# One 128-wide spreading product instead of two 64-wide ones in neighbourhood attention

## The chip, the cores and the metric

The kernel runs on one core of a Trainium2 chip. The metric is the time of one execution in device microseconds (us); three runs of the kernel before give a median of 941.36 us. Besides them one execution was recorded by the hardware profiler; all rows below come from it. Engines are named as in the profile: PE is TensorE's matrix products, PEld its weight loads (the stationary operand), DVE is VectorE, ACT ScalarE, POOL GpSimd, SP SyncE.

## What is computed

Two transformer-like blocks over 512 tokens of width 1024. The second block has two layers; in each, half of the width goes through neighbourhood attention: tokens stand on a grid of 8 rows by 64 columns, and each of 8 heads (head size 64) attends to a window around its token. Cut to what matters:

```python
logits = einsum('bhcd,bhicjd->bhcij', qr, kr) * scale + bias
p = softmax(logits)                      # over the keys of the window
out_a = einsum('bhcij,bhicjd->bhcd', p, vr)
...
y = concatenate([out_a * silu(g_a), out_b * silu(g_b)])
x = x + y @ w_out[l]
```

The kernel does not divide the probabilities by their sum. It weighs the values with the unnormalised exponentials, and multiplies the result, together with the gate, by the reciprocal of the sum. The result has the head's 64 channels on the partitions and 128 tokens along the free axis, while the reciprocals stand as one column of 128 tokens on the partitions. So they have to be turned and repeated over 64 partitions, which an identity product does.

## The kernel before

Neighbourhood attention of one layer is 16 steps `m` (`N_NA` = 16), each a pair of heads for 128 queries and 256 keys (`KW`); `M = 16 * l + m` counts over both layers. Three steps are begun early, inside the projections before; the others run in a software pipeline written out by hand, where turn `j` of each engine holds:

- PE: `na_score(j)`, three products (high and low parts of q and k) for each of two heads; the head size of 64 is contracted, so one head uses the upper 64 rows of the array and the other the lower 64. Then `na_turn(j - 2)`, four 128x128 transposes of the exponentials. Then `na_weigh(j - 3)`: four value products with 64 output columns (two heads, two key halves), a wait on `na_rinv`, and two spreading products, one for each head, also 64 columns wide: the stationary operand is the reciprocal column broadcast to 64, the moving one the identity.
- DVE: `na_take(j)` (adds the bias to the scores, finds the maximum), `na_inverse(j - 1)` (the reciprocals of two sums), and every other turn `na_out`, `na_lo`, `na_hi` (gate times reciprocal times result, and its split in two parts); at j = 6, 8, 10, 12 also `mixT_lo`, a 128x512 subtraction.
- ACT: `na_move(j - 2)` (transposed exponentials out of PSUM), then `na_exp(j)` (two exponentials with their sums).

Everything is ordered by semaphores, each engine running its own list in order. `settle` makes the engine wait for the instruction just issued. An fp32 product of PE, here the value and the spreading products, is two entries in the trace; a transpose is one; a score product, whose operands are fp32r, is one. `soft,v` and `soft,xn_t` are the tiles of the value products, `cons,ring` of the transposes, `cons,small` of the spreading products, `k_hi,q_hi` and its like of the scores. In the trace nearly all products have line 1023, a helper's.

Another part of each layer, differential attention, has scores of the same kind, transposes (line 1364) and value products that are 128 columns wide (`v,soft`).

Of the kernel before, what the change touches and what calls it, by code (L numbers as in the profile page):

```python
# [11 lines left out]
P = 128  # L12
# [3 lines left out]
NH, HD, NG = 8, 64, 2  # L16
# [11 lines left out]
KW = 32 * GROWS  # L28
# [40 lines left out]
def build(nc, io):  # L69
# [8 lines left out]
    with ctx:  # L78
# [3 lines left out]
        def sb2(name, n, dtype=fp32):  # L82
            return second.enter_context(nc.sbuf_tensor(name, [P, n], dtype))
# [4 lines left out]
        def cut(view, **dims):  # L88
            return view.rearrange("p (" + " ".join(dims) + ") -> p " + " ".join(dims), **dims)
# [44 lines left out]
        hT_hi, hT_lo = (cut(sb2(n, KD * T, fp32r)[:, :], k=KD, t=T) for n in ("hT_hi", "hT_lo"))  # L134
        w_hi, w_lo = (cut(sb2(n, 4 * UNIT, fp32r)[:, :], u=4, n=UNIT) for n in ("w_hi", "w_lo"))

        prob2 = cut(ring[:, 0:SLOT], b=8, t=T)
        tanh2 = cut(ring[:, 0:NT * 512], i=NT, f=512)
        raw_w = cut(ring[:, SLOT:2 * SLOT], u=4, n=UNIT)
# [12 lines left out]
        def row(name):  # L152
            return rows[:, ROWS[name][0]:ROWS[name][1]]

        def con(name):
            return cons[:, CONS[name][0]:CONS[name][1]]
# [7 lines left out]
        ident = con("ident")  # L164
# [58 lines left out]
        def stat(n):  # L223
            sm_at[0] += n
            assert sm_at[0] <= 640
            return small[:, sm_at[0] - n:sm_at[0]]
# [10 lines left out]
        ssum = stat(16)  # L237
        rinv = stat(16)
# [89 lines left out]
        def p_raw(n):  # L328
            return piece(ring, n)
# [77 lines left out]
        def na_bank(m):  # L407

            return bank[4 + m // 2 % 2]
# [608 lines left out]
        def _(pe):  # L1018
# [3 lines left out]
            def mm(out, lhsT, rhs, first, last):  # L1022
                return pe.matmul(out, lhsT, rhs, start=first, stop=last)  # L1023


            def times_c(out, w, ks=range(KD)):
                for k in ks:
                    r = k % 4 * 32
                    ins = mm(out[r:r + 32, :], csl_pad[:, k, :], w[:, k, :], k < 4, k >= 4)
                return ins  # L1030
# [9 lines left out]
            for c in range(4):  # L1040
                if c < 2:
# [4 lines left out]
                    for i in range(2 * c, 2 * c + 2):  # L1046
                        pe.wait_ge(S["xn_ready"], i + 1)
                        for b in range(2):
                            if i:
                                pe.wait_ge(S["xT_evac"], 2 * i + b - 1)  # L1050
                            for k in range(4):
                                ins = pe.transpose(bank[6 + b][:, k * P:(k + 1) * P], xn[:, i % 2, (4 * b + k) * P:(4 * b + k + 1) * P], ident)
# [4 lines left out]
                else:  # L1057
                    for n in range(2):
                        pe.wait_ge(ada_late_in[1 + n], 16)
                        ins = times_c(bank[c], ada_late[1], range(4 * n, 4 * n + 4))  # L1060
# [59 lines left out]
            for k in range(KD):  # L1120
                pe.wait_ge(S["h_raw"], k + 1)
                ins = mm(bank[0][:, :], p_raw(0)[:, k, :], hT[:, k, :], k == 0, k == KD - 1)
# [15 lines left out]
            for n in range(8):  # L1138
# [3 lines left out]
                for a in range(4):  # L1142
                    g = 4 * (n % 4) + a
                    ins = pe.transpose(bank[4 + n % 4][:, a * P:(a + 1) * P], src[:, g * P:(g + 1) * P], ident)
# [6 lines left out]
            for n in range(2):  # L1151
                for b in range(4):
                    for a in range(4):
                        g = 8 * a + 4 * n + b
                        ins = mm(bank[4 + n][32 * a:32 * a + SC, b * P:(b + 1) * P], b_st[:, g, :], cl3[:, g, 0:P], True, True)
# [5 lines left out]
            for part, w in enumerate((wi, wr)):  # L1161
                if part:
                    pe.wait_ge(S["kk_evac"], 2)
                for g in range(GP):
                    for two in range(2):
                        ins = mm(bank[6 - 2 * part + g // 8][two * SN:(two + 1) * SN, (g % 8) * NCH:(g % 8 + 1) * NCH],
                                 w[:, g, two * SN:(two + 1) * SN], u_in[:, 2 * g + two, :], True, True)
# [46 lines left out]
            for n in range(4):  # L1214
# [6 lines left out]
                for a in range(8):  # L1221
                    g = 2 * (8 * q + a) + two

                    out = bank[4 + n][:, a * NCH:(a + 1) * NCH]
# [3 lines left out]
                    for half_ in halves:  # L1228
                        ins = mm(out[half_, :], cl3[:, g, SC:SC + P][:, half_], st[:, g, :], False, True)
                ins.then_inc(S["y_done"], 1)  # L1230

            for f in range(4):
# [3 lines left out]
                if f == 2:  # L1236
# [5 lines left out]
                    for m in range(2):  # L1242
                        ins = mm(bank[5][0:64, 0:HD], hk[:, 0, m, :], w2k[:, m, :], m == 0, m == 1)
                    ins.then_inc(S["kc_done"], 1)
                    for g in range(NG):
                        for m in range(2):
                            for h in range(2):
                                half_ = slice(h * SN, (h + 1) * SN)
                                ins = mm(bank[6][half_, g * HD:(g + 1) * HD], vdup[:, m, g, half_], w2v[:, m, :], m == 0, m == 1)
# [47 lines left out]
            for f in range(4):  # L1297
                if 1 <= f < 3:
                    pe.wait_ge(S["proj_evac"], PT_ZA + f)
                out, cs_ = bank[GLU_BANKS[f]][:, :], slice(f * P, (f + 1) * P)  # L1300
# [8 lines left out]
                for k in range(4):  # L1309
                    if f == 0:  # L1310
                        pe.wait_ge(S["h_lower"], KD + k + 1)
                    ins = mm(out, glu_w_hi[:, k, cs_], y_lo[:, k, :], False, k == 3)
# [33 lines left out]
            for n in range(2):  # L1346
                for a in range(4):
                    o = (4 * n + a) * P
                    ins = pe.transpose(bank[n][:, a * P:(a + 1) * P], soft[:, o:o + P], ident)
# [61 lines left out]
            n = len(PAIRS1)  # L1411
# [31 lines left out]
            def tile_T(out, l, g, f):  # L1443

                u = first_unit(l, g) + f
                pe.wait_ge(S["w_split"], u + 1)
                for k in range(KD):
                    w = [unit_shape(v, u)[:, k, :] for v in (w_hi, w_lo)]
                    ins = mm3(out[:, :], w, (hT_hi[:, k, :], hT_lo[:, k, :]), k, k == 0, k == KD - 1)
                return ins  # L1450

            def tile_tok(out, l, g, i, order=range(KD), between=None):

                tok = slice(i * P, (i + 1) * P)
                for m, k in enumerate(order):
                    u = first_unit(l, g) + m // 2
                    if m % 2 == 0 and i == 0:
                        pe.wait_ge(S["w_split"], u + 1)
                    if m == 4 and between:
                        between()  # L1460
                    w = [unit_shape(v, u)[:, m % 2, :] for v in (w_hi, w_lo)]
                    ins = mm3(out[:, :], (hT_hi[:, k, tok], hT_lo[:, k, tok]), w, k, m == 0, m == KD - 1)
                    if m in (1, 3, 5) and i == NT - 1:
                        ins.then_inc(S["w_used"], 1)
                return ins
# [59 lines left out]
            def na_weigh(l, m):  # L1525
                i, p = PAIRS_NA[m]
                M = N_NA * l + m
                pe.wait_ge(S["na_moved"], M + 1)
                if m % 2 == 0 and M >= 4:
                    pe.wait_ge(S["na_out"], M // 2 - 1)  # L1530
                src, b0 = ((v2, 0), (v_mid, 0), (v_mid, 1), (v2, 2))[i]
                out = na_bank(m)
                for b in range(2):
                    for e in range(2):
                        hf = slice(e * HD, (e + 1) * HD)
                        mm(out[hf, m % 2 * P:(m % 2 + 1) * P], src[:, b0 + b, (2 * p + e) * HD:(2 * p + e + 1) * HD],
                           probT2[:, m % 4, e * KW + b * P:e * KW + (b + 1) * P], m % 2 == 0 and b == 0, False)
                pe.wait_ge(S["na_rinv"], M + 1)
                for e in range(2):
                    hf = slice(e * HD, (e + 1) * HD)  # L1540
                    r = (2 * M + e) % 16
                    ins = mm(out[hf, KW + m % 2 * P:KW + (m % 2 + 1) * P], rinv[:, r:r + 1].to_broadcast([P, HD]), ident, False, m % 2 == 1)
                ins.then_inc(S["na_weighed"], 1)

            for l in range(LAYERS):
                for half in (1, 0):
# [15 lines left out]
                    for g in range(4 - 4 * half, 8 - 4 * half):  # L1562
                        for t in range(4):
# [6 lines left out]
                            if KINDS[g] not in BY_TOKENS:  # L1570
                                ins = tile_T(bank[p % 4], l, g, t)
                            elif (g, t) == (0, 1):
                                ins = tile_tok(bank[p % 4], l, g, t, between=lambda: (rows_T(l, 2), rows_T(l, 3)))
                            else:
                                ins = tile_tok(bank[p % 4], l, g, t)
# [3 lines left out]
                            if (g, t) in MIX_TURNS:  # L1579
                                m = MIX_TURNS.index((g, t))  # L1580
# [11 lines left out]
                    if half:  # L1592
                        for j in range(N_EARLY, N_DA + LAG_O):
# [5 lines left out]
                            if LAG <= j < N_DA + LAG:  # L1599
                                m = j - LAG  # L1600
                                turn(u0 + m, prob_of(k0 + 2 * m), NT, "mixed", u0 + m + 1)
                            if j >= LAG_O:
                                m = j - LAG_O
# [32 lines left out]
        def _(dve):  # L1636
            steps = [0]

            def settle(ins):
                ins.then_inc(S["vec_step"], 1)  # L1640
                steps[0] += 1
                dve.wait_ge(S["vec_step"], steps[0])
# [10 lines left out]
            def wide_b(v, n):  # L1653

                return v.unsqueeze(2).to_broadcast([v.shape[0], v.shape[1], n])
# [184 lines left out]
            for l in range(LAYERS):  # L1840
                sl = slice(l * HD, (l + 1) * HD)
                for m, (a, b) in enumerate((("lq1", "lk1"), ("lq2", "lk2"))):
                    ins = dve.tensor_tensor_reduce(kc_sb[:, 0:HD], row(a)[:, sl], row(b)[:, sl], 1.0, 0.0, MUL, ADD,
                                                   lam_t[:, 2 * l + m:2 * l + m + 1])
# [127 lines left out]
            for m in range(2):  # L1972
                ins = dve.tensor_copy(vdup[:, m, :, :].rearrange("p g (u j) -> p g u j", u=4),
                                      src[:, 1, m, :, :].unsqueeze(2).to_broadcast([P, NG, 4, NCMP]))
# [34 lines left out]
            for g in range(NG):  # L2009
                for q in range(4):  # L2010
                    ins = dve.tensor_copy(vblk[q * 32:(q + 1) * 32, g, q * HD:(q + 1) * HD],
                                          bank[6][q * 32:(q + 1) * 32, g * HD:(g + 1) * HD])
# [92 lines left out]
            n = len(PAIRS1)  # L2105
# [129 lines left out]
            def na_inverse(l, m):  # L2235
                M = N_NA * l + m
                dve.wait_ge(S["na_exp"], 2 * M + 2)
                if M >= 8:
                    dve.wait_ge(S["na_weighed"], M - 7)
                r = slice(2 * M % 16, 2 * M % 16 + 2)  # L2240
                dve.reciprocal(rinv[:, r], ssum[:, r]).then_inc(S["na_rinv"], 1)

            def na_out(l, g):
                dve.wait_ge(S["na_weighed"], N_NA * l + 2 * g + 2)
# [16 lines left out]
            for l in range(LAYERS):  # L2261
                for half in (1, 0):
# [75 lines left out]
                    else:  # L2338
                        for j in range(N_EARLY, N_NA):
# [9 lines left out]
                            if j - MIX_LAG in MIX_AT:  # L2349
                                m = MIX_AT.index(j - MIX_LAG)  # L2350
                                mixT_lo(l, m, 4 + m, mixT[m])
                        na_inverse(l, N_NA - 1)
                        for g in range(N_NA // 2 - 2, N_NA // 2):
                            na_out(l, g)
# [118 lines left out]
```

## Time and profile before

| what | value |
|---|---|
| median of three runs | 941.36 us (941.17 to 942.0) |
| the profiled execution, whole | 941.23 us |
| its span, first to last instruction | 939.4 us |
| mean granted TensorE clock | 0.996 |
| neighbourhood attention's pipeline, layer 1 | 564.15 to about 591.8 us |
| the same, layer 2 | 860.75 to about 888.4 us |

The profiled execution is 0.13 us off the median of the others, so sums made against it hold for the median too. The span leaves out 1.8 us before the first and after the last instruction.

A row of the timeline gives start in us, duration in us, engine, line, operation, output and inputs by name, the array mode (rows*columns in use) for PE, the shape, and how many neighbouring entries are merged. For merged entries the duration runs from the start of the first to the end of the last. Ends of products are modelled; starts are what to read. Brackets give idle time before the row and what ended it.

### The profile page before, as it was taken

The page shows a single profiled execution, that of the slowest core. Times are in us where ns is not written, and L with a number is a line of the kernel's source. Part 1 is how long each engine was busy: PE and PEld are TensorE (multiplying, and loading weights), DVE is VectorE, ACT ScalarE, POOL GpSimd, SP SyncE. Part 2 cuts the span into 40 slices and gives each one's busy share as a digit, 9 for nine tenths or more (in the row PEclk, how much of TensorE's full clock was granted, in tenths as well). Part 3 has the DMA queues.
Part 4 walks back from the last instruction along what each step waited for, and adds up shares of the span by engine and source line. Part 5 has one row for each costly group of instructions (what it writes and reads, how often), then busy time and mean ns, then how long its engine had stood idle before and what let it go on. Part 6 is the DMA issues. An engine that isn't in the chain of part 4 may idle for free.

```text
span 939.4 us, 14917 instructions
## 1 busy us (share of the span) xinstructions
PE 906.4 (96%) x5861; PEld 715.3 (76%) x5861; DVE 587.7 (63%) x1200; ACT 450.7 (48%) x962; POOL 70.3 (7%) x89
## 2 busy tenths in 40 slices
PE   3999999999999999999999999999999999999996
PEld 1689888865667788887888877888887788887785
DVE  5899798998886472438862448344255965335733
ACT  4734223666784243436925348233434863436631
POOL 1001130006300010000010000000000010000002
PEclk9999999999999999999999999999999999999999
DMA  9735636266000232332304224122243222333203
GB/s 380 312 109 125 181 136 180 102 209 239 1 2 23 90 129 90 112 101 76 111 8 150 90 90 134 43 90 90 90 155 92 62 91 89 94 100 118 72 0 90
DMA packets 34647, 104.71 MB, mean 111 GB/s; under 512 B 14929, under 2 KB 14929, under 8 KB 32146
## 3 DMA queue, kind: packets, MB, share of 16 engines
q1 hardware_dynamic: 28098, 85.77, 27.5%
q0 software_dynamic: 3824, 15.73, 5.2%
q10 hardware_dynamic: 2656, 2.26, 1.0%
q8 instruction: 47, 0.77, 0.3%
q14 instruction: 22, 0.18, 0.1%
HBM read 98.37 MB, written 4.19 MB: 109 GB/s over the span
## 4 chain that ended last, share of the span: by engine, by line
PE 88%; DVE 6%; ACT 2%; issue 2%; DMA 1%; SPq 0%; POOL 0%; POOLq 0%; DVEq 0%; ACTq 0%
PE bank L1023 81%; PE bank L1384 2%; PE bank L1522 2%; DMA ring<-in_w_ada 1%; PE bank L1364 1%; DVE ring L2083 1%; PE bank L1440 1%; DVE arena L1651 0%; DVE ring L2282 0%; ACT ring L834 0%; PE bank L1430 0%; ACT arena L715 0%; DVE soft L2115 0%; ACT w_hi L882 0%; DVE soft L2093 0%
## 5 line engine op out<-in xcount | busy, mean ns | idle before, releaser
L2138 DVE TENSOR_TENSOR w_lo<-ring,w_hi 128x1024 fp32r<-128x1024 f32 x80 | 97.8, 1225 | 114.6 <-ACT w_hi L882 111.5
L1023 PE MATMUL bank<-w_hi,hT_hi 128*128 128x512 f32 x320 | 125.3, 392 | 1.3 <-issue 1.0
L1023 PE MATMUL bank<-hT_hi,w_hi 128*128 128x512 f32 x320 | 126.3, 395 | 0.0
L1023 PE MATMUL bank<-hT_lo,w_hi 128*128 128x512 f32 x320 | 124.6, 389 | 0.0
L1023 PE MATMUL bank<-hT_hi,w_lo 128*128 128x512 f32 x320 | 124.6, 389 | 0.0
L1023 PE MATMUL bank<-w_lo,hT_hi 128*128 128x512 f32 x320 | 124.6, 389 | 0.0
L1023 PE MATMUL bank<-w_hi,hT_lo 128*128 128x512 f32 x320 | 124.5, 389 | 0.0
L882 ACT ACTIVATE w_hi<-ring 128x1024 fp32r<-128x1024 f32 x80 | 84.4, 1058 | 11.6 <-PE bank L1023 11.4
L1023 PEld LDWEIGHTS bank<-w_hi,hT_hi 128*128 128x128 f32 x320 | 60.1, 188 | 14.7 <-issue 2.6
L1023 PEld LDWEIGHTS bank<-hT_hi,w_hi 128*128 128x128 f32 x320 | 60.1, 188 | 14.0 <-issue 0.7
L1023 PEld LDWEIGHTS bank<-hT_lo,w_hi 128*128 128x128 f32 x320 | 60.1, 188 | 12.8
L1023 PEld LDWEIGHTS bank<-w_lo,hT_hi 128*128 128x128 f32 x320 | 60.1, 188 | 12.6
L1023 PEld LDWEIGHTS bank<-w_hi,hT_lo 128*128 128x128 f32 x320 | 60.1, 188 | 12.2
L1023 PEld LDWEIGHTS bank<-hT_hi,w_lo 128*128 128x128 f32 x320 | 60.1, 188 | 12.0
L887 ACT ACTIVATE bank<-x_t 128x512 f32<-128x512 f32 x24 | 14.4, 602 | 101.5 <-DVE x_t L2363 68.0
L834 ACT ACTIVATE ring<-ring,small 128x512 f32<-128x512 f32 x64 | 45.7, 714 | 14.9 <-DVE small L2083 12.4
L1023 PE MATMUL bank<-arena 128*64 128x64 f32 (+5 forms) x608 | 51.0, 293 | 0.3 <-PE bank L1023 0.2
L2083 DVE CUSTOM_DVE_ANT_0 ring<-bank,bias_ring 128x512 f32<-128x512 f32 x64 | 41.2, 685 | 0.9 <-PE bank L1023 0.9
L1023 PEld LDWEIGHTS bank<-arena 128*64 128x64 f32 (+1 forms) x608 | 31.3, 147 | 11.3 <-issue 10.2
L953 ACT ACTIVATE q_hi<-bank 128x512 fp32r<-128x512 f32 x16 | 9.6, 598 | 60.2 <-PE bank L1023 60.2
L2307 DVE SCALAR_TENSOR_TENSOR q_lo<-bank,q_hi 128x512 fp32r<-128x512 f32 x16 | 11.1, 692 | 43.2 <-ACT q_hi L953 43.2
L2363 DVE TENSOR_TENSOR x_t<-bank,x_t 128x512 f32<-128x512 f32 x16 | 11.0, 690 | 40.1 <-PE bank L1023 40.1
(323 smaller groups left out, 1814.1 us busy)
## 6 DMA issues: line engine op xcount, KB each, us to landing
ring<-in_w_units SPq DMA_DIRECT2D x80, 512.0 KB, 3.6
ring<-in_w_ada SPq DMA_DIRECT2D x4, 2048.0 KB, 10.2
bias_ring<-in_na_bias POOLq DMA_DIRECT2D x8, 1024.0 KB, 5.5
ring<-in_w_out SPq DMA_DIRECT2D x2, 2048.0 KB, 8.7
bias_ring<-in_t_bias POOLq DMA_DIRECT2D x8, 448.0 KB, 3.8
x_t<-in_x SPq DMA_DIRECT2D x4, 512.0 KB, 5.9
arena<-in_w_ada SPq DMA_DIRECT2D x1, 2048.0 KB, 20.3
arena<-in_w_ada SPq DMA_DIRECT2D x2, 1024.0 KB, 23.2
```

What stands on the lines that cost most here:

```text
L834: act.activation(p, p, ACT.Exp, scale=-1.0, bias=negm[:, k % 8:k % 8 + 1], accum_out=ssum[:, k % 8:k % 8 + 1])\
L882: act.activation(w_hi[:, u % 4], raw_w[:, u % 4], ACT.Copy).then_inc(S["w_hi_ready"], 1)
L887: settle(act.activation(place[:, 0:n], x[:, i, c0:c0 + n], ACT.Square, scale=scale, accum_out=ssq[:, part * NT + i:part * NT + i + 1]))
L953: act.activation(q_hi[:, t, :], src[:, :], ACT.Copy, scale=SCALE).then_inc(S["qk_hi"], 1)
L1023: return pe.matmul(out, lhsT, rhs, start=first, stop=last)
L1364: ins = pe.transpose(bank[u % 2][:, b * P:(b + 1) * P], src[:, b * P:(b + 1) * P], ident)
L1384: ins = pe.transpose(bank[k % 2][:, b * P:(b + 1) * P], prob1_of(k)[:, b * P:(b + 1) * P], ident)
L1522: ins = pe.transpose(bank[m % 2][:, at_], prob2[:, m % 8, at_], ident)
L2083: dve.tensor_tensor_reduce(prob_of(k)[:, 0:width], bank[S_BANKS[k % 4]][:, 0:width], bias, -scale, 3.0e38, ADD, MIN, negm[:, k % 8:k % 8 + ...
L2138: dve.tensor_tensor(w_lo[:, u % 4], raw_w[:, u % 4], w_hi[:, u % 4].bitcast(fp32), SUB).then_inc(S["w_split"], 1)
L2307: dve.scalar_tensor_tensor(lo_[:, t, :], bank[(pt2(l, g) + t) % 4][:, :], SCALE if isq else 1.0, hi_[:, t, :].bitcast(fp32), MUL, SUB).the ...
L2363: dve.tensor_tensor(xs, bank[6 + t % 2][:, :], xs, ADD).then_inc(S["x_ready"], 1)
```

## The change

`na_inverse` now waits for its reciprocals and then writes them out 128 wide in a new tile `spread` (four buffers): 64 columns with the first head's, 64 with the second's. `na_weigh` reads these as one 128-column stationary operand, so one product instead of two fills the result's 128 partitions. The wait that guards the buffer goes from 8 steps back to 4.

```diff
+        spread = cut(sb2("spread", 4 * P)[:, :], b=4, n=P)
...
                 pe.wait_ge(S["na_rinv"], M + 1)
-                for e in range(2):
-                    hf = slice(e * HD, (e + 1) * HD)
-                    r = (2 * M + e) % 16
-                    ins = mm(out[hf, KW + m % 2 * P:KW + (m % 2 + 1) * P], rinv[:, r:r + 1].to_broadcast([P, HD]), ident, False, m % 2 == 1)
+                ins = mm(out[:, KW + m % 2 * P:KW + (m % 2 + 1) * P], spread[:, m % 4, :], ident, False, m % 2 == 1)
                 ins.then_inc(S["na_weighed"], 1)
...
                 dve.wait_ge(S["na_exp"], 2 * M + 2)
-                if M >= 8:
-                    dve.wait_ge(S["na_weighed"], M - 7)
+                if M >= 4:
+                    dve.wait_ge(S["na_weighed"], M - 3)
                 r = slice(2 * M % 16, 2 * M % 16 + 2)
-                dve.reciprocal(rinv[:, r], ssum[:, r]).then_inc(S["na_rinv"], 1)
+                settle(dve.reciprocal(rinv[:, r], ssum[:, r]))
+                dve.tensor_copy(cut(spread[:, m % 4, :], e=2, d=HD), wide_b(rinv[:, r], HD)).then_inc(S["na_rinv"], 1)
```

## Rows read from the trace of the kernel before

**Rows 1.** The page: busy time and share of the span by engine.
```profile
PE 906.4 (96%) x5861; PEld 715.3 (76%) x5861; DVE 587.7 (63%) x1200; ACT 450.7 (48%) x962; POOL 70.3 (7%) x89
```

**Rows 2.** The chain that ended last, 545 to 610 us (start, duration, what).
```profile
565.58 0.59 PE bank L1522 x4
...
584.97 0.59 PE bank L1522 x4
...
588.31 0.59 PE bank L1522 x4
...
589.70 0.59 PE bank L1522 x4
```

**Rows 3.** Timeline of PE, one turn of the pipeline.
```profile
577.14 0.66 PE L1522 MATMUL bank<-cons,ring 128*128 128x128 f32 x4
...
577.31 0.49 PE L1522 MATMUL bank<-cons,ring 128*128 128x128 f32 x3
...
577.73 0.66 PE L1023 MATMUL bank<-soft,v 128*64 128x128 f32 x8
578.22 0.39 PE L1023 MATMUL bank<-cons,small 128*64 128x128 f32 x4
578.54 0.38 PE L1023 MATMUL bank<-k_hi,q_hi 64*128 64x256 f32 x2
578.76 0.28 PE L1023 MATMUL bank<-k_hi,q_lo 64*128 64x256 f32 x2
```

**Rows 4.** Timeline of PE in differential attention, 445 to 455 us.
```profile
448.23 0.66 PE L1364 MATMUL bank<-cons,ring 128*128 128x128 f32 x4
448.73 1.06 PE L1023 MATMUL bank<-v,soft 128*128 128x128 f32 x8
449.71 0.51 PE L1023 MATMUL bank<-k_hi,q_hi 64*128 64x512 f32 x2
```

**Rows 5.** Timeline where the pipeline of layer 1 ends, 590 us on.
```profile
591.46 0.39 PE L1023 MATMUL bank<-cons,small 128*64 128x128 f32 x4
591.78 0.50 PE L1023 MATMUL bank<-w_hi,hT_hi 128*128 128x512 f32 x1
...
594.63 0.39 PE L1023 MATMUL bank<-w_hi,hT_hi 128*128 128x512 f32 x1
...
593.35 0.42 DVE L2258 TENSOR_TENSOR hT_lo<-y,hT_hi 128x256 fp32r<-128x256 f32 x1
```

**Rows 6.** Timeline of DVE, two turns of the pipeline in layer 2.
```profile
874.26 0.42 DVE L2231 CUSTOM_DVE_ANT_0 ring<-bank,bias_ring 128x256 f32<-128x256 f32 x1
...
875.03 0.67 DVE L2143 TENSOR_TENSOR hT_lo<-y,hT_hi 128x512 fp32r<-128x512 f32 x1
875.93 0.42 DVE L2231 CUSTOM_DVE_ANT_0 ring<-bank,bias_ring 128x256 f32<-128x256 f32 x1 [0.23 <-PE bank L1023]
...
878.01 0.42 DVE L2231 CUSTOM_DVE_ANT_0 ring<-bank,bias_ring 128x256 f32<-128x256 f32 x1
```

**Rows 7.** Timeline of DVE in differential attention: two reciprocals, the second waited for.
```profile
436.71 0.16 DVE L2278 RECIPROCAL small<-small 128x1 f32<-128x1 f32 x1
436.79 0.15 DVE L2279 RECIPROCAL small<-small 128x1 f32<-128x1 f32 x1
436.97 0.22 DVE L1651 SCALAR_TENSOR_TENSOR small<-small 128x1 f32<-128x1 f32 x1
```

**Rows 8.** DVE groups by line and shape (busy us, mean ns): 128 columns.
```profile
L2093 DVE TENSOR_SCALAR arena<-arena,small 128x128 f32<-128x128 f32 x8 | 2.4, 345 | 0.1
```

**Rows 9.** Timeline of ACT: the end of step 12's exponentials.
```profile
583.13 0.19 ACT L940 ACTIVATION_READ_ACCUMULATOR ring<-ring,small 128x1 f32 x1
```

**Rows 10.** Timeline of the weight loads, the turn of rows 3.
```profile
578.53 0.19 PEld L1023 LDWEIGHTS bank<-k_hi,q_hi 64*128 64x128 f32 x2 [0.17 <-DVE small L2231]
```

**Rows 11.** Weight loads grouped by line and shape (busy us, mean ns of one).
```profile
L1522 PEld LDWEIGHTS bank<-cons,ring 128*128 128x128 f32 x128 | 13.4, 140 | 5.2 <-DVE k_lo L2307 1.0 <-ACT soft L947 0.7
L1023 PEld LDWEIGHTS bank<-cons,small 128*64 128x64 f32 x128 | 8.1, 137 | 0.0
```

## The prediction

> **What bounds the kernel now.** I read the page first: PE is busy 96% of the span, DVE 63%, no other engine more than that [rows 1]. Then the chain that ended last, in the stretch of neighbourhood attention. It is made of PE's products alone. The transposes of step 2 begin at 565.58 and those of step 12, ten turns on, at 584.97, so a turn takes 1.94 us; the last two transposes, with no more scores in the turn, begin at 588.31 and 589.70, 1.39 apart [rows 2]. Layer 2 looks the same. So in both layers this stage costs what PE's own list costs, and a nanosecond more or less per turn on PE goes straight into the time. DVE is fuller here than its average says, and has to be looked at too.
>
> The third view is PE's timeline, and there the starts, not the lengths. I read one turn [rows 3]. A merged row's last start is its start plus its length less the 0.27 us of a single product. The transposes start at 577.14, 577.31 and then every 0.11 to 577.53. The eight value entries begin at 577.73; the last of their four pairs starts at 578.12. The four spreading entries begin at 578.22, and their last pair at 578.34. The scores begin at 578.54.
>
> Two readings carry the prediction. **First**, the 64-wide products run two at a time: eight entries take four slots of 0.11 us (577.73 to 578.12), four take two (578.22, 578.34). The two heads' products lie in different column halves of the array, and share a slot. **Second**, whenever the array mode in the row changes (64\*128, 128\*128, 128\*64), time is lost twice. The next start comes 0.20 us after the last one in place of 0.11 (577.53 to 577.73, 578.34 to 578.54), and the second slot after the switch comes late too (577.14 to 577.31 is 0.17; 578.54 to 578.76 is 0.22). Between value and spreading products, both 128\*64, nothing is lost: 578.12 to 578.22. Nor is anything lost in differential attention between transposes and value products, which are both 128\*128: the last transpose starts at 448.62 and the first value product at 448.73; but its scores then start 0.20 after the last value product [rows 4].
>
> **The change on PE.** Two products become one; four entries become two.
>
> What the two entries cost: differential attention's value products are the same kind, fp32, 128 columns wide and 128 moving columns. Eight of them take 1.06 us [rows 4], less 0.27 or 0.28 for the last, over seven intervals: 0.11 us each. So the merged product takes two slots of 0.11, as the two half-wide ones did together. Halving the number of products saves nothing in the array, because the two already shared it.
>
> What the switch costs: a turn now goes 64\*128 (scores), 128\*128 (transposes), 128\*64 (values), 128\*64 (spreading), back to scores, three switches. With the change spreading is 128\*128, and there are four. From the last pair of value products at 578.12: before, 0.10 + 0.12 + 0.20 = 0.42 us to the scores. After: 0.20 for the switch, 0.17 to the second entry (as after the switch into the transposes), 0.20 for the switch into the scores, which is what leaving 128\*128 costs in [rows 4]: 0.57 us. The difference is 0.15 us.
>
> How often: steps 0 to 11 are followed by scores, 12 in each layer. Steps 12 and 13 are followed by transposes. There the extra switch is not extra: spreading and transposes are then one mode, so the switch only moves ahead of the spreading. Before: 0.11 + 0.11 + 0.20 + 0.17 to the second transpose; after: 0.20 + 0.17 + 0.11 + 0.11: the same. Step 14 is followed by the value products of step 15, the same mode before, another after: one more time 0.15. Step 15 is followed by the 128\*128 products with the output weights, at the same switch of 0.32 us after the first spreading entry (591.46 to 591.78) [rows 5], which again only moves. So 13 times per layer, 26 in all, 26 x 0.15 = 3.9 us. Bounds for one: the first start's delay alone is 0.10, and with the larger second-slot delay, that of the scores (0.11), it is 0.21: 2.6 to 5.5 us.
>
> The Trainium skill, TensorEngine Tiling (Array Packing), section Key Properties, says that changing the tiling mode, not just the tile, drains TensorE. The trace agrees, by the 0.20 us in place of 0.11 at each change of mode. By that rule, too, this change adds one drain to a turn; the page gives no price for it.
>
> **The change on DVE.** A reciprocal that nobody waits for is followed 0.08 us later by the next instruction (436.71 to 436.79); waited for, it takes 0.18 (436.79 to 436.97) [rows 7]: 0.10 more. Then the copy of 128x128, broadcast from two columns. The trace has no such copy. It should cost at least the 0.08 of the smallest instruction, and at most the 0.34 of a 128x128 TENSOR_SCALAR, which does two operations [rows 8]. I take 0.20, about halfway. So 0.30 more per step, 0.18 to 0.44.
>
> Is it hidden? In the fullest two turns DVE works from 874.26 to 875.70 (with the 128x512 subtraction) and from 875.93 to 878.01, 3.52 us [rows 6], in a PE time of 3.88. With 2 x 0.30 it is 4.12, in a PE time that has itself become 2 x 2.09 = 4.18. At the upper bound it is 4.40: 0.22 behind per two turns, four times in a layer, 0.9 us. What is late then is the scores' pick-up, ACT's exponentials behind it, and the transposes behind those. Step 12's exponentials end at 583.32 [rows 9], and its transposes begin at 584.97 [rows 2]: 1.6 us of slack, more than 0.9. The reciprocals are needed later still: step j's is made in turn j + 1 and used in turn j + 3. So DVE's part costs nothing, and it would cost only if the copy took over 0.42 us: then 0.4 or more is lost in each two turns and the slack of 1.6 is used up after four.
>
> The shortened guard (4 steps back, not 8) waits for step M - 4 to be weighed. DVE comes to it after it has taken the scores of step M + 1, which PE issues after that very weighing. It never waits. At the first three steps of a layer there is no such step in flight. Nothing is moved past a queue, and no DMA is added.
>
> At the layer's end, DVE's last split ends at 593.77, and PE needs it at its thirteenth product, 594.63 [rows 5]: 0.86 us of room. The switch that moves ahead of the last spreading takes some 0.2 of it. Covered.
>
> **Sum.** 941.23 + 3.9 = 945.1 us (the median stands 0.13 higher, which I leave out). A difference under 0.2%, 1.9 us, can't be told from none.
>
> **Rivals.**
>
> - *The switch costs as read.* 943.8 to 946.7 us by the bounds. Chance 0.71.
> - *The switch is mostly hidden.* The idle time at a switch may belong to the neighbour that is left (64\*128 or the waits around it) and not to each change. For it: the profile puts the 0.17 us in which the weight loads stand still before the scores down to DVE [rows 10]. Against it: the same 0.20 stands before the value products, and at 128\*64 to 128\*128, 591.46 to 591.78 [rows 5]. With 0 to 0.07 us each: 941.2 to 943.1, all of it no measurable change. Chance 0.14.
> - *DVE becomes the bound.* The copy takes over 0.42 us, say 0.6: two turns are 3.52 + 1.40 = 4.92 on DVE against 4.18, 0.74 behind, four times 3.0, less 1.6 of slack, 1.4 per layer: 945.1 + 2.8 = 947.9. Range 945.5 to 948. Against it: the longest row of that width is 0.34 [rows 8]. Chance 0.08.
> - *Faster: the wide product is cheaper than two half ones.* It would have to take one slot, not two, or load its weights quicker: 0.11 saved, 32 times, 3.5 us, 937.7. It decides as soon as the saving is above the switch, so only if the switch costs nothing as well. Against it: 0.11 per entry in [rows 4]. The Trainium skill, TensorEngine Tiling (Array Packing), Restrictions, says that column tiling rules out Fast Weight Load, so the wide load could gain. In the trace a 128-wide load takes 140 ns and a 64-wide one 137 [rows 11], so no such gain shows. Chance 0.07.
>
> **How the numbers follow.** Prediction 945.1, the likeliest case. The first case holds 0.71; DVE's case below 947.4 adds some 0.06, and the upper third of the hidden case, from 942.4, adds 0.05: 942.4 to 947.4 holds 0.82. Slower is the first case and DVE's, 0.79; no measurable change is the hidden one, 0.14; faster is the last, 0.07.
>
> **What the changed profile would show.** PE's turn at 2.09 us, not 1.94, the chain still PE alone; the spreading row x2, 128\*128, starting 0.20 after the last value pair; the scores 0.37 after it, not 0.32. The last two turns still 1.39 apart. On DVE a copy of about 0.2 us, and the exponentials still over 1 us ahead of their transposes. If the turn stays at 1.94, the switch reading was wrong; if the chain passes through DVE, its cover was.

## The result, and the profile after

The change made the kernel slower: 947.72 us (median of 4 runs, 946.44 to 948.23) against 941.66 of the kernel before beside it, a ratio of 1.0063 with a 95% interval of 1.0045 to 1.008. That is 6.1 us; forecast were 3.9, in a range that ended at 947.4. A second comparison in more rounds (below) gave 946.46 against 941.17 us, 1.0061 (1.0047 to 1.0075).

The page of the changed kernel's profiled execution, busy time by engine, answers to [rows 1]:

```profile
span 946.4 us, 14825 instructions
PE 913.7 (97%) x5797; PEld 718.4 (76%) x5797; DVE 595.0 (63%) x1232; ACT 451.8 (48%) x962; POOL 70.2 (7%) x89
```

PE has 64 entries fewer (5797, not 5861) and is busy 7.3 us longer. This execution took 948.23 us, the longest of its four; its span is 7.0 us over that of before.

The chain that ended last, 545 to 615 us (start, duration, what), answers to [rows 2]:

```profile
566.27 0.59 PE bank L1523 x4
566.86 1.55 PE bank L1024 x16
568.41 0.59 PE bank L1523 x4
569.00 1.55 PE bank L1024 x16
570.55 0.59 PE bank L1523 x4
...
589.81 0.59 PE bank L1523 x4
590.40 1.01 PE bank L1024 x10
591.40 0.44 PE bank L1523 x4
591.84 1.01 PE bank L1024 x10
592.85 0.44 PE bank L1523 x4
```

The chain is still PE alone. A turn takes 2.14 us (568.41 to 570.55), not 1.94 as in [rows 2], and the eleven from 566.27 to 589.81 are all alike. The last two transposes are 1.45 apart, not 1.39.

PE's timeline, one turn, answers to [rows 3]; behind it the timeline of the weight loads in it, which answers to [rows 10]:

```profile
579.04 0.66 PE L1523 MATMUL bank<-cons,ring 128*128 128x128 f32 x4
579.63 0.66 PE L1024 MATMUL bank<-soft,v 128*64 128x128 f32 x8
580.22 0.49 PE L1024 MATMUL bank<-cons,spread 128*128 128x128 f32 x2
580.63 0.38 PE L1024 MATMUL bank<-k_hi,q_hi 64*128 64x256 f32 x2
580.86 0.28 PE L1024 MATMUL bank<-k_hi,q_lo 64*128 64x256 f32 x2
```

```profile
579.63 0.42 PEld L1024 LDWEIGHTS bank<-soft,v 128*64 128x64 f32 x8 [0.17 <-issue]
580.21 0.30 PEld L1024 LDWEIGHTS bank<-cons,spread 128*128 128x128 f32 x2 [0.17 <-issue]
```

The last value pair starts at 579.63 + 0.66 - 0.27 = 580.02. The spreading entry follows 0.20 later (before: 0.10), with an idle 0.17 in the loads that was not there before. The second entry comes 0.22 after the first (0.49 less 0.27), and the scores 0.19 after that. From the last value pair to the scores it is 0.61 us, and was 0.42.

The tile view of the new tile: duration of one in ns, least, median and most, then first and last start.

```profile
L1024 PEld LDWEIGHTS bank<-cons,spread x64: 186/188/189, 565.2 to 895.2; 128*128 128x128 f32 x64
...
L2240 DVE COPY spread<-small x32: 226/227/229, 554.2 to 892.8; 128x128 f32<-128x128 f32 x32
its engine sat idle before it (us, times) until:
  issue: 5.5, 32
```

The idle time of 5.5 us, 32 times (0.17 each), is that of the weight loads at the switch ahead of each of the 32 spreading products.

DVE's timeline, two turns of layer 1, answers to [rows 6]:

```profile
575.20 0.41 DVE L2229 CUSTOM_DVE_ANT_0 ring<-bank,bias_ring 128x256 f32<-128x256 f32 x1
...
575.88 0.16 DVE L2239 RECIPROCAL small<-small 128x2 f32<-128x2 f32 x1
576.08 0.23 DVE L2240 COPY spread<-small 128x128 f32<-128x128 f32 x1
576.22 0.68 DVE L2141 TENSOR_TENSOR hT_lo<-y,hT_hi 128x512 fp32r<-128x512 f32 x1
577.14 0.42 DVE L2229 CUSTOM_DVE_ANT_0 ring<-bank,bias_ring 128x256 f32<-128x256 f32 x1 [0.24 <-PE bank L1024]
...
579.50 0.42 DVE L2229 CUSTOM_DVE_ANT_0 ring<-bank,bias_ring 128x256 f32<-128x256 f32 x1
```

The copy starts 0.20 us after the reciprocal, and the next instruction 0.14 after the copy; a step costs DVE 0.34 where it cost 0.08. Two turns of work are 1.70 + 2.36 = 4.06 us in a PE time of 4.28, and DVE still waits for PE once in them.

Over the whole, the parts are these. Up to the second product with the output weights (592.12 before, 595.37 after) layer 1 is 3.25 us later, but 0.49 of it was there before the stage began (the chain's `ACT k_hi` piece at 562.55, before at 562.06), so the stage itself gained 2.76. Layer 2's stage begins 4.19 us later (862.86, before 858.67), 0.94 more than layer 1's end explains, and gains the same again. So 5.5 us lie in the two stages, and 1.4 of this execution's 7.0 in stages that the change doesn't touch: the 0.49, and the 0.94 between the layers' stages. The windows of both traces show where the 0.94 lies:

```profile
700.00:750.00 50.00, 48.91 (x255) 37.70 (x254) 32.36 (x83) 26.56 (x59) 1.16 (x2) 0.97 0.31 92
```

Columns: the stretch, its length, busy time with counts of PE, PEld, DVE, ACT and POOL, PE's granted clock, DMA share and GB/s. Here in layer 2's differential attention the granted clock is 0.97, where it was 1.00 before: from 738.7 on, 3.4 us ran at 1.2 GHz, and the rest at 2.4 GHz. In the 8 us ahead of it PE was busy for 6.93, in both traces. The other traces fit this. In the four with such a stretch near 740 us (this one, e2, e6, e10), layer 2's stage begins 267.5 to 267.6 us after the second product with layer 1's output weights; in the seven without it, 266.6.

### The profile page after: what moved, and what is told of

It reads as the page before. It is cut to its first block, busy times and chain, and to the rows that moved or that the text cites. A ratio compares the mean times of both kernels' runs of the same rounds, so it can differ in the third digit from the quotient of the medians.

```text
span 946.4 us, 14825 instructions
## 1 busy us (share of the span) xinstructions
PE 913.7 (97%) x5797; PEld 718.4 (76%) x5797; DVE 595.0 (63%) x1232; ACT 451.8 (48%) x962; POOL 70.2 (7%) x89
## 3 DMA queue, kind: packets, MB, share of 16 engines
HBM read 98.37 MB, written 4.19 MB: 108 GB/s over the span
## 4 chain that ended last, share of the span: by engine, by line
PE 86%; DVE 7%; issue 3%; ACT 3%; DMA 1%; SPq 0%; POOL 0%; POOLq 0%; DVEq 0%; ACTq 0%
PE bank L1024 80%; PE bank L1385 2%; DVE ring L2081 2%; PE bank L1523 2%; DMA ring<-in_w_ada 1%; DVE ring L2281 1%; PE bank L1365 1%; PE bank L1441 1%; ACT ring L835 1%; DVE arena L1649 0%; DVE small L1649 0%; PE bank L1431 0%; ACT arena L716 0%; DVE soft L2113 0%; ACT w_hi L883 0%
```

## The experiments

Code is quoted against the kernel before or the changed one, as each says. The time before is that of the runs beside it: 941.34 us for the first four, 941.17 for the next three, 941.01 for the last two.

**e1: the vector engine's part alone.** Against the changed kernel:

```diff
-                ins = mm(out[:, KW + m % 2 * P:KW + (m % 2 + 1) * P], spread[:, m % 4, :], ident, False, m % 2 == 1)
+                for e in range(2):
+                    hf = slice(e * HD, (e + 1) * HD)
+                    ins = mm(out[hf, KW + m % 2 * P:KW + (m % 2 + 1) * P], spread[:, m % 4, hf], ident, False, m % 2 == 1)
```

> The changed kernel with its vector-engine part kept (the waited-for reciprocal, the 128-wide copy, the guard 4 steps back) and the two 64-wide spreading products back, which now read the two halves of the copy. If the extra array mode switch is the cost: the turn is 1.94 us again and the time that of the kernel before, 941 to 942.3 us. If the vector engine's copy and wait are the cost: it stays at 946 to 948 us, and the chain passes through DVE.

Measured: 940.96 us, ratio 0.9997 (0.9988 to 1.0006). PE's timeline:

```profile
577.60 0.39 PE L1024 MATMUL bank<-cons,spread 128*64 128x128 f32 x4
577.92 0.39 PE L1024 MATMUL bank<-k_hi,q_hi 64*128 64x256 f32 x2
...
579.54 0.39 PE L1024 MATMUL bank<-cons,spread 128*64 128x128 f32 x4
```

The turn is 1.94 us. The wait for the reciprocal, the copy and the nearer guard are hidden: together they cost nothing that this comparison can see.

**e2: the wide product alone.** Against the kernel before; both heads are divided by the first head's sum:

```diff
-                for e in range(2):
-                    hf = slice(e * HD, (e + 1) * HD)
-                    r = (2 * M + e) % 16
-                    ins = mm(out[hf, KW + m % 2 * P:KW + (m % 2 + 1) * P], rinv[:, r:r + 1].to_broadcast([P, HD]), ident, False, m % 2 == 1)
+                r = 2 * M % 16
+                ins = mm(out[:, KW + m % 2 * P:KW + (m % 2 + 1) * P], rinv[:, r:r + 1].to_broadcast([P, P]), ident, False, m % 2 == 1)
```

> The kernel before with nothing changed on the vector engine, but one 128-wide spreading product whose stationary operand is the first head's reciprocal broadcast to 128 columns, so the second head's result is divided by the first head's sum. If the switch is the cost: a turn of 2.14 us and 946 to 948 us, as the changed kernel. If the vector engine is the cost: 941 to 942.3 us.

Measured: 946.98 us, ratio 1.0059 (1.0046 to 1.0072), and a turn of 2.14 us. The whole loss, with nothing changed on DVE.

**e3: the same wide product, ahead of the values.** Against the changed kernel: in `na_weigh` the wait on `na_rinv` and the wide product (with `start` on even `m`) stand before the value products, which then carry the `stop`.

```diff
+                pe.wait_ge(S["na_rinv"], M + 1)
+                mm(out[:, KW + m % 2 * P:KW + (m % 2 + 1) * P], spread[:, m % 4, :], ident, m % 2 == 0, False)
                 for b in range(2):
...
-                pe.wait_ge(S["na_rinv"], M + 1)
-                ins = mm(out[:, KW + m % 2 * P:KW + (m % 2 + 1) * P], spread[:, m % 4, :], ident, False, m % 2 == 1)
```

> The changed kernel with the 128-wide spreading product moved ahead of the value products, right behind the 128-wide transposes, so that a turn has three mode switches again, with the same products. If the switch is the cost: a turn of 1.94 us and 941 to 942.5 us. If the wide product itself costs more than the two narrow ones, or the copy: 945 to 948 us.

Measured: 942.32 us, ratio 1.0008 (0.9999 to 1.0017). PE's timeline:

```profile
577.82 0.66 PE L1523 MATMUL bank<-cons,ring 128*128 128x128 f32 x4
578.31 0.39 PE L1024 MATMUL bank<-cons,spread 128*128 128x128 f32 x2
578.63 0.66 PE L1024 MATMUL bank<-soft,v 128*64 128x128 f32 x8
579.21 0.39 PE L1024 MATMUL bank<-k_hi,q_hi 64*128 64x256 f32 x2
...
580.25 0.39 PE L1024 MATMUL bank<-cons,spread 128*128 128x128 f32 x2
```

The same entries with the same operands, and a turn of 1.94 us. Behind the transposes the first starts 0.11 after the last of them, and the second 0.12 later (0.39 less 0.27). The stages hold the 1.0 us that is left, 0.49 in each layer. In the last turn step 15's product has no transposes ahead of it and stands between values, between two switches of its own:

```profile
591.72 0.49 PE L1024 MATMUL bank<-cons,spread 128*128 128x128 f32 x2
```

That is 0.25. In the first turn PE waits for ACT ahead of the values anyway, and the product stands behind that wait; that is 0.20.

**e4: two more switches.** Against the changed kernel, the wide product stands between the value products of the two key halves:

```diff
                 for b in range(2):
                     for e in range(2):
...
+                    if b == 0:
+                        pe.wait_ge(S["na_rinv"], M + 1)
+                        mm(out[:, KW + m % 2 * P:KW + (m % 2 + 1) * P], spread[:, m % 4, :], ident, False, False)
-                pe.wait_ge(S["na_rinv"], M + 1)
-                ins = mm(out[:, KW + m % 2 * P:KW + (m % 2 + 1) * P], spread[:, m % 4, :], ident, False, m % 2 == 1)
```

> The changed kernel with the 128-wide spreading product between the value products of the two key halves: the same products again, five mode switches in a turn. If each switch costs what the first one did, 0.2 us: a turn of about 2.34 us; one switch more in each of the 32 steps adds 6.4 us, 953 to 955 us. If the cost is not that of switching: 947 to 948 us.

Measured: 952.35 us, ratio 1.0115 (1.0101 to 1.0128), 11.0 us over the kernel before. The chain:

```profile
572.69 0.59 PE bank L1523 x4
573.28 1.71 PE bank L1024 x16
574.99 0.59 PE bank L1523 x4
```

A turn of 2.30 us, not the 2.34 expected, and a time below the 953 to 955 expected: a miss on the size. The first additional switch costs 0.20, the second 0.15. It is the second that leads back into narrow products.

**e5: the changed kernel again**, unaltered.

> The changed kernel once more, in more rounds, beside the kernel before on the same chip. The turns explain 2.5 us in a layer until the scores run out and 0.3 at its end, 5.5 us together; the rest of the first comparison (6.1 us between the medians, 7.0 between the profiled runs) lies in other stages. If it belongs to the change, it is 6 to 7 us again; if it is the scatter of those stages from run to run, 5.0 to 6.0 us.

Measured: 946.46 us (945.81 to 948.37, 5 runs), ratio 1.0061 (1.0047 to 1.0075). The medians are 5.3 us apart, and the ratio gives 5.7. The turns are 2.14 us again. Layer 2's stage begins at 861.13 in this trace, 2.46 us after that of before. In the first comparison it was 4.19, with the same stage code. So the 1.4 us outside the stages come and go between executions of one kernel. This trace has no stretch at 1.2 GHz before the kernel's end.

The recorded mean clocks sort the runs of both kernels in the same way. Of the changed kernel's nine, the four at 0.997 or 0.998 took 945.8 to 946.5 us, and the five at 0.994 or 0.995 took 947.5 to 948.4. Of the 46 of the kernel before beside the experiments, the seven at 0.994 took 942.0 to 943.3, the others 940.3 to 941.9. Three of the first comparison's four runs of the changed kernel were of the longer kind, which is why its median is high. Why they are 5 of 9 there and 7 of 46 before, and whether the change has a part in that, no run shows.

**e6: two extra switches without any wide spreading product.** Against the kernel before, `na_turn(j - 2)` is split: its two transposes of head 0 before `na_weigh(j - 3)`, those of head 1 between its value and its two narrow spreading products.

```diff
                             if j < N_NA + 2:
-                                na_turn(l, j - 2)
-                            na_weigh(l, j - 3)
+                                na_turn(l, j - 2, (0,))
+                                na_weigh(l, j - 3, lambda: na_turn(l, j - 2, (1,)))
```

> The kernel before, with no wide product at all, but with the two transposes of the second head put between a step's value products and its two narrow spreading products: two more mode switches in a turn, into 128*128 by a load of 140 ns and back into 128*64 by one of 137 ns. If the second start behind a switch is late by what the new weight load takes (0.05 us for these, 0.11 for the 188 ns of the wide spreading load), each costs 0.15 us: a turn of 2.24 us. If every switch costs what the changed kernel's cost, 0.20: a turn of 2.34 us. Whole: 949 to 952 us.

Measured: 952.02 us (2 runs), ratio 1.0114 (1.0095 to 1.0132). PE's timeline:

```profile
576.83 0.39 PE L1023 MATMUL bank<-k_hi,q_hi 64*128 64x256 f32 x2
...
578.34 0.44 PE L1522 MATMUL bank<-cons,ring 128*128 128x128 f32 x2
578.71 0.44 PE L1023 MATMUL bank<-cons,small 128*64 128x128 f32 x4
579.07 0.39 PE L1023 MATMUL bank<-k_hi,q_hi 64*128 64x256 f32 x2
```

The turn is 2.24 us, as worked out from 0.15 for a switch with a short load behind it; the whole is at the upper end of the 949 to 952 expected. 0.30 us more a turn in the 12 turns with scores, twice, is 7.2 us. The rest of the 10.9 lies at the layers' ends, where in this order the last products wait for ACT (the chain has a piece `ACT soft` there); I didn't take it apart further. The narrow spreading products take 0.44, not 0.39, right behind a switch: their second pair, too, starts 0.16 to 0.17 behind the first, 0.05 late.

**e7: fewer switches.** Against the kernel before, PE's list in batches of two steps (its start, up to the transposes of step 1, is left out here); on DVE `na_out`, `na_hi`, `na_lo` and `mixT_lo` move by one turn.

```diff
+                        for j in range(4, N_NA + 4, 2):
+                            if j < N_NA:
+                                na_score(l, j)
+                                na_score(l, j + 1)
+                            if j < N_NA + 2:
+                                na_turn(l, j - 2)
+                                na_turn(l, j - 1)
+                            na_weigh(l, j - 4)
+                            na_weigh(l, j - 3)
```

> The kernel before with TensorE's list in batches of two steps: scores of two, transposes of two, value and narrow spreading products of two, so three switches per two steps, not six; the vector engine's gate work and low parts move by one turn to fit. If switches cost 0.15 to 0.21 each, a batch takes PE 3.4 us, not 3.88, with ScalarE near its limit at 3.0 to 3.5: about 3 us less per layer, 935 to 939 us. If the loss at a switch is only waiting, 941 to 942 us.

Measured: 939.85 us, ratio 0.999 (0.9981 to 0.9999). It is about 1 us below the kernel before, and not 3 us a layer as expected: a miss. Loads and DVE in its timelines:

```profile
573.70 0.42 DVE L2235 CUSTOM_DVE_ANT_0 ring<-bank,bias_ring 128x256 f32<-128x256 f32 x1 [1.54 <-DMA bias_ring<-in_na_bias]
576.60 0.19 PEld L1023 LDWEIGHTS bank<-k_hi,q_hi 64*128 64x128 f32 x2 [1.36 <-DVE small L2235]
...
581.46 0.20 PEld L1522 LDWEIGHTS bank<-cons,ring 128*128 128x128 f32 x2 [0.23 <-ACT ring L940]
```

Where the others keep up, a batch takes 3.44 us (scores from 868.25 to 871.69 in layer 2; the batches around it take 3.49 to 3.65), against 3.88 for two turns. In layer 1 DVE, which picks up the scores, waits 1.54 us for the bias to land, and PE's loads 1.36 for DVE; elsewhere transposes wait for exponentials. The gain at the switches is there in layer 2, whose stage, from ACT's `k_hi` piece to the second product with the output weights, is 1.1 us shorter than before (28.93 for 30.05). In layer 1 (30.31) other waits take more than it gives.

**e8: the changed kernel in these batches**, with eight buffers for the copies, where 938 to 941 us were expected, gave no time: `spread` needed 4096 bytes of each partition, and 2080 were left. e10 takes its place, with four buffers.

**e9: the batches with ACT's list reordered**, the exponentials of both steps ahead of both moves, against e7:

```diff
+                        for j in range(4, N_NA + 2, 2):
+                            for k in (j, j + 1):
+                                if k < N_NA:
+                                    na_exp(l, k)
+                            na_move(l, j - 2)
+                            na_move(l, j - 1)
```

> The batches of two steps with narrow products (as e7_batch_narrow), and ScalarE's list changed to fit: in a batch the exponentials of both steps first, then the two moves of transposed tiles, so that no transposes wait for exponentials. If those waits (seen in e7's chain: up to 0.3 us at the transposes of a batch, 2.7 us of ScalarE in the chain at a layer's end) hid the gain: batches at 3.4 us of PE and 936 to 938.5 us. If ScalarE's own load is the limit: about 940 us, as e7.

Measured: 943.68 us, ratio 1.0029 (1.0018 to 1.0041). A miss: slower than before, where 936 to 938.5 or about 940 were expected. Its loads show one thing that is late now, the moves that free the transposes' banks:

```profile
871.63 0.42 PEld L1526 LDWEIGHTS bank<-cons,ring 128*128 128x128 f32 x4 [0.61 <-ACT soft L947]
```

In layer 2 the chain runs through something else, the transfer of a bias,

```profile
863.80 7.68 DMA bias_ring<-in_na_bias
```

and for which DVE waits 0.53 us at 871.50. The price of each alone was not measured.

**e10: the changed kernel's copy and wide product in those batches**, both wide products behind the values of two steps, the reciprocals one turn later:

```diff
+                            na_value(l, j - 4)
+                            na_value(l, j - 3)
+                            na_spread(l, j - 4)
+                            na_spread(l, j - 3)
```

> The same batches and ScalarE order with the changed kernel's copy and wide product: value products of two steps, then the two wide spreading products (the reciprocals are made one turn later, so that four buffers are enough). If the change's cost is one more mode switch: 0.20 us per batch, 13 to 16 of them in two layers, so 2.5 to 3.5 us above the batched narrow kernel, and still below the kernel before or level with it. If the wide product or the copy costs by itself: 5 us or more above.

Measured: 948.43 us, ratio 1.0075 (1.0062 to 1.0089), 4.8 us above e9 where 2.5 to 3.5 were expected. Part of that is the clock: e10's profiled run has the stretch at 1.2 GHz near 740 us, and e9's has not. The two stages together grew by 3.8 us. The chain in layer 1 says why even that doesn't measure the switch:

```profile
579.03 0.23 DVE spread L2254
579.26 0.34 DVE y L1657
...
583.01 0.23 DVE spread L2254
583.24 0.34 DVE y L1657
...
587.01 0.23 DVE spread L2254
```

The chain passes through DVE and its copies, one batch in 4.0 us, about the 4.06 that DVE's two turns of work take in the changed kernel. So with PE's list shorter DVE bounds this stretch, and the copy is on the chain. In layer 2 a bias transfer of 8.7 us stands on the chain ahead of it. How e10's loss divides between copy, switch and transfer is not shown.

## Why the prediction was wrong in size and right in mechanism

**What bounds it: right.** The chain is PE alone in both stages, and time goes 1:1 into the span.

**No saving from one product for two: right.** Two narrow products share a slot; the wide one takes 0.11 to 0.12 per entry in e3 and leaves the turn at 1.94 us.

**One more mode switch: right, and shown.** The loss is there without DVE's part (e2) and gone without the wide product (e1). It is gone too with the wide product and one switch fewer (e3), and grows by 0.15 us with another (e4). e6 produces it without any wide spreading product.

**What a switch costs: the step that failed.** The working said "After: 0.20 for the switch, 0.17 to the second entry (as after the switch into the transposes), 0.20 for the switch into the scores". The measured interval to the second entry is 0.22, so that a step costs 0.20 us more and not 0.15. I had taken the delay behind the switch into transposes for a property of mode 128\*128. The rows say it goes with the weight load: behind loads of 185 to 188 ns (scores, and now the spreading product) the second start is 0.10 to 0.11 us late, behind those of 140 and 137 ns (transposes, values) 0.05 to 0.06 [rows 3, 11]. The trace of before showed it in mode 128\*128 itself, where the products with the output weights, whose loads take 188 ns, follow the switch at 591.78 [rows 5]:

```profile
592.12 0.40 PE L1023 MATMUL bank<-w_hi,hT_lo 128*128 128x512 f32 x1
592.35 0.39 PE L1023 MATMUL bank<-w_lo,hT_hi 128*128 128x512 f32 x1
```

The second starts 0.34 behind the first, the third 0.23 behind the second. Within one mode neither delay shows: in e3 the same spreading entries follow one another after 0.12, where they take 0.22 behind a switch. There the loads run under the products before, and behind a switch they have stood still. e6, with only short loads behind its extra switches, came out at 0.15 each as reckoned by that rule, one of them the same change from 128\*64 to 128\*128 that costs 0.20 with the spreading product behind it; e4's pair came out at 0.20 and 0.15. Whether the load's length itself does it, or something else that goes with this kind of product, no run separates. My upper bound, 0.21, came from just this row of the scores, and was the better value.

**How often: nearly right.** The stage gained 2.76 us a layer: 12 x 0.20, 0.05 to 0.06 for each of the two steps followed by transposes (taken at nothing: 1.45 for 1.39), and 0.25 between steps 14 and 15, where 0.15 stood. Two layers make 5.5 us, so 946.7 for 941.2. e5's median is 0.2 below that. The first comparison's 947.72 is 1.0 above it, by the runs with the lower mean clock; for those the forecast had no term.

**DVE hidden: right.** Estimated were 0.30 us more a step, and it is 0.26; two turns are 4.06 us where 4.12 was expected, and e1 shows that it costs nothing. The rival in which DVE becomes the bound didn't happen here, but it did in e10's layer 1, once PE's batches were shorter.

**The other rivals.** The switch was not hidden; and nothing in the wide product was cheaper, its load is 188 ns and a narrow one 137.

The Trainium skill, TensorEngine Tiling (Array Packing), Key Properties, says that changing the tiling mode drains TensorE. The runs agree that each change costs time, 0.15 to 0.20 us for each added one in the changed kernel, e4 and e6; that it is a drain they do not show.

## What to carry to other kernels

Read the array mode in TensorE's rows before merging narrow products: if two 64-wide ones already share a slot, a 128-wide one saves nothing, and it may bring a mode switch where none was. Count switches per turn, and price each by the start that comes late and by the second start behind it, taken from a row with a weight load of the same length. The cheap remedy is order: put the product next to others of its mode, which took the loss away but gained nothing (e3), or batch steps, which gained about 1 us (e7); but then look again at the engines that were just keeping up.

## What the runs showed that I had not expected

- A mode switch costs 0.20 us with a 188 ns load behind it and 0.15 with one of 137 to 140 ns, of which 0.10 is the late first start. A batch of two steps gets back 0.44 us of 3.88 at best.
- A DVE copy of 128x128 fp32 broadcast from two columns takes 0.227 us, and the next instruction starts 0.14 us after the copy's start.
- DVE's wait for a bias in layer 1 was 0.3 us before and is 1.5 in e7, where its consumer comes earlier.
- 3.4 us at 1.2 GHz in layer 2's differential attention go with 0.9 to 1.0 us more there, in the changed kernel as in e2, e6 and e10.
